# Weight sums of a Strassen-Winograd feed-forward moved into the down stretch, and one activation copy moved behind the next gate's first product

## What is computed

```python
def block_out(x, pool_o, attn_o, w_out, norm_ffn, w_gate, w_up, w_down):
    h = x + jnp.concatenate([pool_o, attn_o], axis=-1) @ w_out
    hn = rms_norm(h, norm_ffn)
    return h + (jax.nn.silu(hn @ w_gate) * (hn @ w_up)) @ w_down
```

## Time and profile before

| | |
|---|---|
| median of 3 runs | 2406.07 us (2400.6 to 2410.79) |
| the profiled execution | 2410.94 us, its span 2409.1 us |
| TensorE busy | 2189.3 us, 91% of the span, 11991 matmuls |
| VectorE, ScalarE, GpSimd busy | 62%, 39%, 40% |
| mean granted TensorE clock | 0.968 of full speed |
| DMA | 160 MB, 66 GB/s in the mean |

### The profile page before, as it was taken

The page is one execution under the profiler, slowest core; times in us unless marked ns, Lnnn a source line. Parts: engine busy times, 40 slices in busy tenths (PEclk is TensorE's granted clock), DMA queues, the critical chain, the costliest instruction groups (busy, mean ns, idle before and its releaser), DMA issues.

```text
span 2409.1 us, 34470 instructions
## 1 busy us (share of the span) xinstructions
PE 2189.3 (91%) x11991; PEld 1931.4 (80%) x11991; DVE 1487.3 (62%) x2372; ACT 939.3 (39%) x2070; POOL 971.0 (40%) x629
## 2 busy tenths in 40 slices
PE   7999899999999899998999999998998888898887
PEld 7866788888888798767888888887975677787886
DVE  4558566656566545675665656656368567666675
ACT  4665433322232336644332223333475333232331
POOL 2312344444454222124554444542412355455452
PEclk9999999999999999999999999999999898998988
DMA  4121021231112331111123111222412022313122
GB/s 128 44 71 36 18 71 53 61 95 53 52 52 72 106 138 45 53 36 36 53 63 94 53 52 52 67 73 98 127 44 71 24 71 71 87 52 102 55 62 66
DMA packets 194387, 160.04 MB, mean 66 GB/s; under 512 B 7005, under 2 KB 176906, under 8 KB 194282
## 3 DMA queue, kind: packets, MB, share of 16 engines
q1 hardware_dynamic: 191326, 149.58, 21.3%
q10 hardware_dynamic: 2956, 9.08, 1.0%
HBM read 149.66 MB, written 9.07 MB: 66 GB/s over the span
## 4 chain that ended last, share of the span: by engine, by line
PE 32%; issue 29%; POOL 16%; DVE 15%; ACT 6%; DMA 2%; POOLq 0%; DVEq 0%; SPq 0%; ACTq 0%
POOL ring_lo L620 14%; PE ps L775 10%; PE ps L776 9%; PE ps L777 9%; DVE s_sb L1806 2%; DVE negmax L1811 2%; ACT s_sb L1348 2%; DMA raw<-in_w_up 2%; POOL w_lo L620 1%; DVE st L1905 1%; PE ps L789 1%; DVE h L1647 1%; DVE st L1897 1%; PE ps L882 1%; DVE act_lo L1961 1%
## 5 line engine op out<-in xcount | busy, mean ns | idle before, releaser
L620 POOL TENSOR_TENSOR ring_lo<-raw,ring_hi 128x512 fp32r<-128x512 f32 (+1 forms) x276 | 410.1, 1487 | 692.0 <-ACT ring_hi L1214 625.3
L775 PE MATMUL ps<-xt_hi,ring_hi 128*128 128x384 f32 (+1 forms) x1152 | 389.1, 338 | 48.7 <-POOL ring_lo L620 44.6
L1647 DVE TENSOR_TENSOR h<-ps,h 128x512 f32<-128x512 f32 (+1 forms) x476 | 316.2, 685 | 181.9 <-PE ps L777 180.5
L776 PE MATMUL ps<-xt_lo,ring_hi 128*128 128x384 f32 (+1 forms) x1152 | 383.2, 333 | 0.0
L777 PE MATMUL ps<-xt_hi,ring_lo 128*128 128x384 f32 (+1 forms) x1152 | 382.5, 332 | 0.0
L620 POOL TENSOR_TENSOR ring_lo<-st,ring_hi 128x512 fp32r<-128x512 f32 x198 | 284.9, 1452 | 171.5 <-ACT ring_hi L1214 170.9
L775 PE MATMUL ps<-w_hi,act_hi 128*128 128x512 f32 x704 | 285.5, 406 | 31.9 <-DVE w_lo L1994 17.3
L775 PE MATMUL ps<-tx,ring_hi 128*128 128x384 f32 (+1 forms) x792 | 263.3, 332 | 50.9 <-DVE uu L1931 49.5
L620 POOL TENSOR_TENSOR w_lo<-raw,w_hi 128x1024 fp32r<-128x1024 f32 x66 | 172.5, 2616 | 330.7 <-ACT w_hi L1193 318.4
L776 PE MATMUL ps<-w_lo,act_hi 128*128 128x512 f32 x704 | 282.0, 401 | 0.0
L777 PE MATMUL ps<-w_hi,act_lo 128*128 128x512 f32 x704 | 281.8, 400 | 0.0
(11 more groups left out here) (209 smaller groups left out, 4264.8 us busy)
## 6 DMA issues: line engine op xcount, KB each, us to landing
raw<-in_w_gate SPq DMA_DIRECT2D x66, 512.0 KB, 7.5
raw<-in_w_up SPq DMA_DIRECT2D x66, 512.0 KB, 5.3
raw<-in_w_down SPq DMA_DIRECT2D x66, 512.0 KB, 3.3
raw<-in_w_in SPq DMA_DIRECT2D x33, 512.0 KB, 3.9
raw<-in_w_out SPq DMA_DIRECT2D x24, 512.0 KB, 4.4
h<-in_x_prompt SPq DMA_DIRECT2D x16, 512.0 KB, 7.4
out<-h ACTq DMA_DIRECT2D x16, 512.0 KB, 2.7
xload<-in_x_prompt SPq DMA_DIRECT2D x10, 512.0 KB, 6.2
```

What stands on the lines that cost most here:

```text
L620: nc.gpsimd.tensor_tensor(lo, raw, hi.bitcast(F32), ALU.subtract).then_inc(done, 1)
L775: nc.tensor.matmul(out, w_hi, m_hi, start=first, stop=False, skip_group_check=onto)
L776: nc.tensor.matmul(out, w_hi, m_lo, start=False, stop=False, skip_group_check=onto)
L1647: nc.vector.tensor_tensor(out, ps[0:rows, bank, :], out, ALU.add).then_inc(d_free, 1)
```

## The change

Gate and up get sum buffers of their own (`st[:, 0]` and `st[:, 1]`), two each: S5 and S6, and S4 is written over S6 once S6 is split. S4 has a semaphore of its own (`s4_ready`), and the scratch of the second statistics moves from `uu` to `st[:, 1]`. `combine_weights` on VectorE becomes `weight_sum(s, j, which, n)` with one sum per call. S5, S6, S7 of the next gate are placed between the down additions, behind tiles 1, 2, 3; S4 of the gate opens the group; S5, S6, S7 of up are placed between t and C22 of the gate; S4 of up follows the last down addition. On GpSimd group 0's gate has three sums in place of four. The high part of block (1,0) moves on ScalarE into the next group, behind that group's first weight copy, and its low part on VectorE behind S4. The split of down block c=1 becomes the function `down_low`. In the last group of a part the down blocks are split at products 10 and 11 instead of 12 and 13, and `down_low` follows the low part of block (1,1). SyncE's list is not changed.

```diff
-DOWN_AT = (12, 13)
+DOWN_AT, DOWN_AT_LAST = (12, 13), (10, 11)
...
-            st = sb("st", [PART, 3, HALF], scope=ffn)
-            uu = sb("uu", [PART, D_MODEL], scope=ffn)
+            st = sb("st", [PART, 2, 2, HALF], scope=ffn)
+            uu = sb("uu", [PART, TMAX], scope=ffn)
...
@@ high_product on ScalarE
                 if p in S_ORDER:
-                    act.wait_ge(s_ready, 4 * m + S_ORDER[p])
+                    act.wait_ge(s_ready, 3 * m + S_ORDER[p])
+                elif p == 3:
+                    act.wait_ge(s4_ready, m + 1)
...
@@ group on ScalarE
-                    if n in DOWN_AT:
-                        c = DOWN_AT.index(n)
+                    if n == 0:
+                        act_high(s, j - 1, (1, 0))
+                    if n in (DOWN_AT_LAST if last else DOWN_AT):
+                        c = n % 2
...
-                    if block:
-                        (silu if which == 0 else act_high)(s, j, block)
+                    if block and which == 0:
+                        silu(s, j, block)
+                    elif block and (p != 4 or last):
+                        act_high(s, j, block)
...
@@ on VectorE
+            def weight_sum(s, j, which, n):
                 m = s.m0 + 2 * j + which
                 a, b = raw2[:, 2 * which], raw2[:, 2 * which + 1]
+                first, second = st[:, which, 0], st[:, which, 1]
+                if n == 1:
                     for c in range(2):
                         dve.wait_ge(raw2_loaded[2 * which + c], 16 * (USES2 * s.p + 2 + j))
+                    need(dve, split2, low_done(s, j - 1, which, 3) if not (isinstance(j, int) and j == 0) else 0)
+                    nc.vector.tensor_tensor(first, b[:, 0:HALF], b[:, HALF:], ALU.add).then_inc(s_ready, 1)
+                elif n == 2:
+                    dve.wait_ge(s_ready, 3 * m + 1)
+                    nc.vector.tensor_tensor(second, first, a[:, 0:HALF], ALU.subtract).then_inc(s_ready, 1)
+                elif n == 3:
                     nc.vector.tensor_tensor(b[:, 0:HALF], a[:, 0:HALF], b[:, 0:HALF], ALU.subtract)\
                         .then_inc(s_ready, 1)
+                else:
+                    dve.wait_ge(split2, low_done(s, j, which, 6))
+                    nc.vector.tensor_tensor(second, a[:, HALF:], second, ALU.subtract).then_inc(s4_ready, 1)
...
@@ group on VectorE
                 first = isinstance(j, int) and j == 0
-                for part in ("U2", "t", "C22"):
+                weight_sum(s, j, 0, 4)
+                if not first:
+                    act_low(s, j - 1, (1, 0))
+                sums(s, j, 0, "U2")
+                sums(s, j, 0, "t")
+                for n in (1, 2, 3):
+                    weight_sum(s, j, 1, n)
+                for part in ("C22", "C12", "C21"):
                     sums(s, j, 0, part)
-                combine_weights(s, j, 1, 0)
-                sums(s, j, 0, "C12")
-                combine_weights(s, j, 1, 1)
-                sums(s, j, 0, "C21")
-                if not first:
-                    accumulate(s, OUT_GROUPS + j - 1, odd)
+                for t in range(s.nt):
+                    if not first:
+                        accumulate_tile(s, OUT_GROUPS + j - 1, odd, t, t)
+                    if 1 <= t <= 3 and not last:
+                        weight_sum(s, j + 1, 0, t)
+                weight_sum(s, j, 1, 4)
                 for part in ("U2", "t", "C22"):
                     sums(s, j, 1, part)
                 gated(s, j, (1, 1))
-                if not last:
-                    combine_weights(s, j + 1, 0, 0)
                 gated(s, j, (0, 0))
                 act_low(s, j, (1, 1))
+                if last:
+                    down_low(s, j, last)
                 sums(s, j, 1, "C12")
                 gated(s, j, (0, 1))
-                if not last:
-                    combine_weights(s, j + 1, 0, 1)
                 act_low(s, j, (0, 0))
-                act_low(s, j, (0, 1))
                 sums(s, j, 1, "C21")
                 gated(s, j, (1, 0))
-                act_low(s, j, (1, 0))
+                act_low(s, j, (0, 1))
+                if last:
+                    act_low(s, j, (1, 0))
+                else:
+                    down_low(s, j)
```

More of the change, by code:

```diff
@@ L333, in build @@
         xn = raw2[:, 0:2]
-        stats1, stats2 = st.rearrange("p a n -> p (a n)")[:, 0:D_MODEL], uu
+        stats1, stats2 = (st[:, n].rearrange("p a n -> p (a n)") for n in range(2))
         tt = raw1.rearrange("p b n -> p (b n)").rearrange("p (a n) -> p a n", a=4)
@@ L396, in build @@
         s_ready = sem("s_ready")
+        s4_ready = sem("s4_ready")
         tt_ready = sem("tt_ready")
@@ L429, in left @@
             a, b = raw2[:, 2 * which], raw2[:, 2 * which + 1]
-            return {1: a[:, 0:HALF], 2: a[:, HALF:], 3: st[:, 2], 4: b[:, HALF:], 5: st[:, 0], 6: st[:, 1],
-                    7: b[:, 0:HALF]}[product]
-        S_ORDER = {5: 1, 6: 2, 7: 3, 3: 4}
+            return {1: a[:, 0:HALF], 2: a[:, HALF:], 3: st[:, which, 1], 4: b[:, HALF:], 5: st[:, which, 0],
+                    6: st[:, which, 1], 7: b[:, 0:HALF]}[product]
+        S_ORDER = {5: 1, 6: 2, 7: 3}
         def right(s, product):
@@ L648, in combine_weights @@
             def combine_weights(s):
-                st_ = [st[:, n] for n in range(3)]
                 a, b = raw2[:, 0], raw2[:, 1]
@@ L653, in combine_weights @@
                     pool.wait_ge(raw2_loaded[c], 16 * (USES2 * s.p + 2))
[L654 to L656 removed]
+                nc.gpsimd.tensor_tensor(st[:, 0, 0], b[:, 0:HALF], b[:, HALF:], ALU.add).then_inc(s_ready, 1)
+                pool.wait_ge(s_ready, 3 * s.m0 + 1)
+                nc.gpsimd.tensor_tensor(st[:, 0, 1], st[:, 0, 0], a[:, 0:HALF], ALU.subtract).then_inc(s_ready, 1)
                 nc.gpsimd.tensor_tensor(b[:, 0:HALF], a[:, 0:HALF], b[:, 0:HALF], ALU.subtract)\
                     .then_inc(s_ready, 1)
[L659 to L660 removed]
             def windows(s, b):
@@ L743, in body @@
                     number = first
+                    down_at = DOWN_AT_LAST if last else DOWN_AT
                     for n in range(PRODUCTS):
@@ L749, in body @@
                             low_product(*(order + GROUP)[target], q, number)
-                        if n in DOWN_AT:
+                        if n in down_at:
                             number = number + 1
-                            if n == DOWN_AT[0]:
+                            if n == down_at[0]:
                                 low1(DOWN_ID, number)
@@ L1979, in group, with down_low @@
                 gated(s, j, (1, 1))
-                if not last:
-                    combine_weights(s, j + 1, 0, 0)
                 gated(s, j, (0, 0))
                 act_low(s, j, (1, 1))
+                if last:
+                    down_low(s, j, last)
                 sums(s, j, 1, "C12")
                 gated(s, j, (0, 1))
-                if not last:
-                    combine_weights(s, j + 1, 0, 1)
                 act_low(s, j, (0, 0))
-                act_low(s, j, (0, 1))
                 sums(s, j, 1, "C21")
                 gated(s, j, (1, 0))
-                act_low(s, j, (1, 0))
+                act_low(s, j, (0, 1))
[3 more added lines that the diff above has]
+                    down_low(s, j)
+            def down_low(s, j, last=False):
                 dve.wait_ge(hi_done, HI_BLOCKS * s.p + HI_FFN + (PRODUCTS + 2) * (j + 1) - (SLOTS if last else 0))
```

12 lines of the change are left out of this document (removed).

## The result

| | before | after |
|---|---|---|
| median | 2406.47 us (2400.6 to 2410.79) | 2504.61 us (2503.27 to 2505.56) |
| ratio to before | | 1.0409, 95% interval 1.0386 to 1.0432 |
| the profiled execution, its span | 2410.94 us, 2409.1 us | 2503.27 us, 2501.4 us |
| mean granted TensorE clock | 0.968 | 0.954 |

A forecast was written before the change was run, and what follows sets the result against it. TensorE runs back to back, so only its waits count. From 2410.9 us profiled, 96 (parts 1, 2) plus 24 (part 3) less 19 (ends) gave 2512, less 4.9 to the median 2507, stated as 2510 us; range 2430 to 2590.

The forecast's parts named there:

- Product 4 and the groups: Product 4 starts 18.0 us after its group's first gate product; 2.5 us later in parts 1 and 2, 0.1 in part 3.
- What the change takes away: Waits at products 7 and 2 go in parts 1, 2; product 4 could start 12.7 us after first gate product (T).
- Rival (d): Up blocks land by T+10, so product 4 never waits: 2251 us; chance 0.05.
- The split: VectorE's split of the second down block, delayed by turns with GpSimd, ends at T+7.0; bounds T+5.2 and T+9.3.
- rival (c): VectorE waits only for GpSimd's first-down-block split (w_lo); its own split ends T+5.2, product 4 T+16.2: 2384 us; chance 0.10.
- a sharing of the bandwidth: Alternative to VectorE and GpSimd taking turns on the SBUF port: the split would come near T+5.
- The load: On SyncE's queue, up blocks land 8.3 us after the second down block's split ends, at T+15.3.
- The ends: At each part's end the 5.8 us wait becomes 1.7; with 2.3 us of clock, three times, 19 us saved.
- The clock: The 5.3 us gap ahead of product 4 lowers TensorE's clock behind it, costing 2.3 us per group.
- upper bound of 3.4: Most that the lowered TensorE clock was to cost per group behind product 4's gap, in us; lower bound nothing.
- Rival (a): Same wait at product 4, but TensorE's clock holds through a 5 us gap: 2438 us; chance 0.15.
- S4 "free by a hair": Gate's S4 opens the group near T+8.2; copy and split end by T+10.3, before product 3 at T+10.6: no cost.

## Why the prediction was right

It gave 2510 us, and the median is 2504.61; the direction, the place and the mechanism are those of the forecast. Two of its readings were off, and their effects stayed small, in part by luck (under "Product 4 and the groups"). Step by step:

**What the change takes away.** Product 7 and 2 without a wait in parts 1 and 2, product 4 due at T+12.7: confirmed by the kernel with C22 ahead, where product 4 does start at T+12.7. Rival (d), 2251 us, is nearly that kernel (2277.48). Its rest is part 3, where I had product 4 at T+9.9 and it is near T+12.9, because products 7, 2 and 3 wait there for C21 and for GpSimd's low parts; 10 x 3.0 = 30 us against a difference of 26 us.

**The split.** Forecast w_lo's end at T+3.2, gated (1,0) at T+3.7, the low part at T+5.3, the split at T+7.0 (T+7.6 if behind GpSimd's second low part). In the rows above: 490.96, 491.37, 492.94, 495.17, so T+3.2, T+3.6, T+5.2 and T+7.4. The pair of low parts on GpSimd ended at 494.09 and the split 1.1 us later, behind the second one. That is the turn-by-turn pattern; a split that waited for w_lo alone (rival (c)) did not come. The order that I weighed against a sharing of the bandwidth shows in two more places: the sums beside GpSimd take 1.08 to 1.76 us against 0.69 alone, and GpSimd's low part 1.88 us against 1.29. The Trainium skill (SBUF — State Buffer, section "SBUF: two separate sides") says that whichever of the two starts first holds the shared ports for its whole instruction and the other blocks; these runs agree, in both directions.

**The load.** Forecast 8.3 us from the split's end to the landed blocks; in the group above 504.03 - 495.17 = 8.9 us. The term was sound, with a spread that I had not given: in the 23 groups of the kernel after where the trace names the load as what ended VectorE's wait, the split ends at T+7.4 to T+7.5, but the blocks land 7.2 to 9.4 us behind it. So the spread of the wait at product 4, 153.7 / 30 = 5.1 us in the mean and 6.6 at its longest, is the load's.

**Product 4 and the groups.** The gap was forecast at 5.3 us and is 5.1 in the mean. The forecast added 4.8 us per group in parts 1 and 2 and 2.4 in part 3. First matmuls of the first and last of nine equal groups in part 1, and in part 3 of the first and ninth (before) or the first and eighth (after), before:

```profile
372.16 0.34 PE L775 MATMUL ps<-xt_hi,ring_hi 128*128 128x384 f32 x1
...
769.75 0.34 PE L775 MATMUL ps<-xt_hi,ring_hi 128*128 128x384 f32 x1
...
1989.79 0.30 PE L775 MATMUL ps<-xt_hi,ring_hi 128*128 128x288 f32 x1
...
2337.64 0.30 PE L775 MATMUL ps<-xt_hi,ring_hi 128*128 128x288 f32 x1
```

and after:

```profile
378.92 0.34 PE L774 MATMUL ps<-xt_hi,ring_hi 128*128 128x384 f32 x1
...
811.41 0.34 PE L774 MATMUL ps<-xt_hi,ring_hi 128*128 128x384 f32 x1
...
2067.39 0.30 PE L774 MATMUL ps<-xt_hi,ring_hi 128*128 128x288 f32 x1
...
2385.52 0.30 PE L774 MATMUL ps<-xt_hi,ring_hi 128*128 128x288 f32 x1
```

A group of part 1 went from 397.59 / 8 = 49.7 to 432.49 / 8 = 54.1 us, one of part 3 from 347.85 / 8 = 43.5 to 318.13 / 7 = 45.4. That is +4.4 and +2.0 us, so 20 x 4.4 + 10 x 2.0 = 108 us where I had 120 (part 2, read in the same way, goes from 49.9 to 54.4 us). The sum was 12 us high in the groups.

These 12 us do not lie in product 4's start. It comes at T+18.1 in the mean of parts 1 and 2 (forecast T+18.0) and at T+17.7 in part 3. They lie behind it: what follows product 4 became 1.8 us longer in parts 1 and 2 and 1.5 us in part 3, where the forecast had 2.3. Most of the difference is a term that the forecast left out. Before, the groups lost some 0.4 us each behind product 4 to waits of TensorE for tile additions, and the change took that away: this wait fell from 28.7 us to 16.5 in all. The forecast had put the 28.7 us down mostly to start-up, and had said that nothing on TensorE stood behind VectorE's wait for the up blocks; but the tile additions stand behind it in VectorE's list. That the blocks' coming sooner is what took these waits away was not tested by itself.

In part 3 the sum came out near with luck. The T+17.9 of the earlier trace rows is one group of nine that lie between T+15.75 and T+18.2, 17.3 in the mean. And the forecast charged part 3 the gap of parts 1 and 2, 5.3 us, although by the T+9.9 of its own rival (d) the gap would have been 8.1 us. It was 4.7, because product 4 is due there only at T+12.9.

**The ends.** I had 19 us for the three. Alone they gave 15: behind the earlier split a wait for a low part is left, 9.9 / 3 = 3.3 us instead of the 1.7 that I took. 108 - 15 = 93 us against 92.3 between the two profiled executions' times.

**The clock.** Forecast 2.3 us lost behind each gap. With C22 ahead the kernel is 227 us faster, of which the vanished wait is 153.7; the other 73 us, 2.4 per group, are TensorE work that ran slower: its busy time is 2214.3 us with the wait and 2141.3 without it. The most that a group lost behind product 4, against the same stretch with C22 ahead, is 2.8 us; for the forecast's upper bound of 3.4 no row was given, and no run came to it. Rival (a), where the clock holds through the gap, would have been 2438 us and is refuted by the 0.57 behind product 4. How much a shorter gap costs I did not say, and the runs show it in the mean: with a wait of 107.0 / 30 = 3.6 us per group the rest is (2440.84 - 2277.48 - 107.0) / 30 = 1.9 us, with 60.5 / 30 = 2.0 us (the up loads ahead) (2356.94 - 2277.48 - 60.5) / 30 = 0.6 us.

**S4 "free by a hair".** In parts 1 and 2 product 3 does not wait. In part 3 it does, 0.6 to 0.8 us, and product 2 1.5 us, hidden behind the wait at product 4 in the kernel after and visible with C22 ahead (22.9 us in all). That a late S4 would be hidden was in the forecast; that product 2 stays late in part 3 was not.

## What to carry to other kernels

Before an instruction that waits for a transfer is put ahead of one that has all its inputs, ask who waits for the second one: here a sum of 0.56 us behind such a wait cost 227 us, and moved ahead of it the same change became 5% faster than the kernel before. The transfer's time is read from the queue that issues it, not from its size: a load behind another load that waits for a semaphore lands behind that semaphore, here 7 to 9 us after it, so the instruction that raises it (the split) belongs to the path. And when a wait hides other work, as it hid the weight sums' turns with GpSimd, taking the wait away returns less than moving the waiting instruction, here 148 of 227 us, so move the work too.

## What the runs showed of the hardware beyond the forecast

An operation of GpSimd's loses to VectorE as well as the other way: a low part of 128x512 takes 1.29 us alone and 1.88 us when it starts while VectorE is in an operation with two inputs in SBUF; with the loads moved, two of them beside three weight sums took 3.43 us, and the sums 4.5 instead of 2.1. And the clock did not follow from the length of a wait alone. A wait of TensorE of 4 to 6.6 us ahead of product 4, once in each of the groups 1 to 10 in the kernel after, was followed each time by matmuls at the lower clock: over the next 5.4 us the granted clock was 0.50 to 0.74 in all 27 groups whose starts I read. In the kernel with the up loads ahead, all fourteen waits of 1.76 us left it at 1.00, of four waits of 1.81 us two left it there and two were followed by 0.68, and of nine waits of 2.50 us in part 3 five left it at 1.00 and four were followed by 0.68 to 0.73. These are the 5.4 us behind two such waits of 2.50 and 2.49 us:

```profile
1964.18:1969.58 5.40, 5.40 (x28) 4.68 (x29) 2.06 (x4) 2.90 (x7) 3.80 (x3) 1.00 0.24 69
2005.65:2011.05 5.40, 5.40 (x22) 4.67 (x23) 1.37 (x3) 2.96 (x7) 3.76 (x3) 0.68 0.22 66
```

What decides between the two is not shown by these runs.
